# Odd gate and up slabs of the experts: one column group in three one-pass products, six weight slots instead of eight

## The chip, the cores and the metric

The kernel runs on one core of one Trainium2 chip. The metric is the time of one execution on the device in microseconds (us); the median of three executions of the kernel before is 1552.05 us. TensorE (PE) does the matrix products, ScalarE (ACT) and VectorE (DVE) the element-wise work, GpSimd (POOL) some of that and the gathers, and SyncE (SP) issues the weight transfers.

## The reference: what is computed

Two decoder layers over 272 tokens of width 1024. Layer 0 is sliding-window attention and a dense SwiGLU, layer 1 RWKV-7 time mixing and top-2-of-8 SwiGLU experts. The change is in the experts:

```python
def swiglu(t, w_gu, w_down):
    gu = t @ w_gu
    gate, up = jnp.split(gu, 2, axis=-1)
    return (jax.nn.silu(gate) * up) @ w_down

for e in range(N_EXPERTS):                       # 8 experts
    out = out + gates[:, e:e + 1] * swiglu(t, w_gu[e], w_down[e])   # 1024 -> 2 x 3584 -> 1024
```

## The kernel before, in words

The experts run one after the other over at most 96 tokens each, gathered beforehand into `x_all` (the features on the partitions). The 96 tokens are three blocks of 32 (`BLOCKS`). A block's 32 tokens are the stationary operand, so a product fills a strip of 32 columns of TensorE, a **column group** here, and four products that go to the four groups (`quad(j)`, j = 0 to 3) can run beside each other. The weights are the moving operand. All products of the experts are plain float32. In the trace a float32 product shows as two records, each with its own load of the stationary operand; a product of type float32r shows as one.

The weights of one expert come in 24 slabs of 1.8 MB (`BIG`): 16 gate and up slabs (four phases of four slabs: gate and up of the first half of the hidden width, then of the second), and 8 down slabs. A gate or up slab holds two chunks of 128 features (`c`) by four pieces of 448 columns. For each chunk and each block of tokens there are four products, 128x448, one for each column group; I call this a **step**. So a slab has six steps, 24 products and 48 records. Down slabs are multiplied by `hid_T` in products of 256 columns.

The slabs land in `BIG_SLOTS = 8` slots, four in `ring` and four in `arena`. SP issues the load of slab n as soon as slab n - 8 has been multiplied (`big_used`). PE waits for `big_loaded` of the slab's slot. After a gate phase ACT takes the sigmoid (L1687) and DVE multiplies it by the gate (L1773), after the up phase DVE multiplies by up (L1773, `rows_set`) and transposes (L2324, `hidT_set`). In the last expert the 8 down slabs are all resident and are multiplied block by block (`by_block`, L1387), so that the rows of one block are moved out while the next is multiplied; before its end DVE adds the gathered rows of the other experts (`add_rows`, L2278), whose fetches POOL issues (L694), the second one only after `add_rows(0)`.

The engines' queues are in program order, written out by hand; waits stand in the queue where the code has them. L1326 is the helper `pieces` that issues every product of the experts.

Of the kernel before, what the change touches and what calls it, by code (L numbers as in the profile page):

```python
# [20 lines left out]
F32, I32 = mybir.dt.float32, mybir.dt.int32  # L21
# [172 lines left out]
def build(nc, A, OUT):  # L194
    ctx = ExitStack()
    with ctx:
        def sb(name, shape, dtype=F32):
            return ctx.enter_context(nc.sbuf_tensor(name, shape, dtype))
# [136 lines left out]
        otm = [otm, carve(OV + 512 * 23, KC, CH)]  # L335


        x_all = sb("x_all", [P, KC, EXPERTS * CAP])
        hid_T = sb("hid_T", [P, GROUPS, BLOCKS, PIECE])
        hn_hi = sb("hn_hi", [P, TT, D], F32R)  # L340
# [34 lines left out]
        tri = places[:, PASSES * CAP:PASSES * CAP + P]  # L375

        BIG_AT = ARENA - IN_ARENA * BIG
        assert WORK_AT + taken[0] <= BIG_AT and IN_ROWS * BIG <= 2 * TT * D
# [35 lines left out]
        hidT_set = sem("hidden_T_set")  # L414
        big_loaded = [sem(f"expert_slab_loaded{j}") for j in range(BIG_SLOTS)]
        big_used = sem("expert_slab_multiplied")
        hn_ps, hn_hi_set, hn_split = sem("tokens_T_in_psum"), sem("tokens_T_rounded"), sem("tokens_T_split")
        x_ps, x_kept_a, x_kept_v = sem("gathered_in_psum"), sem("gathered_kept_by_scalar"), sem("gathered_kept_by_vector")
        s_early, s_const = sem("vectors_and_eye_loaded"), sem("consts_loaded")
# [280 lines left out]
        def _(pe):  # L700
# [618 lines left out]
            def expert(o, q, e, stored=False):  # L1319
                by_block = e == LAST  # L1320

                def pieces(out, x, w, first, last, blocks=range(BLOCKS)):

                    for b in blocks:
                        for j, piece in w:
                            mm = pe.matmul(out(j, b), x(b), piece, start=first(b), stop=last, skip_group_check=True)  # L1326
                    return mm

                def quad(j):
                    return slice(BLK * j, BLK * (j + 1))  # L1330

                def gate_or_up(i, w):
                    phase, bank = i // PH, 3 * (i // PH % 2)
                    if i == PH:
                        if not e:
                            pe.wait_ge(put_kept, 2 * o + 2)
                        elif not stored:
                            pe.wait_ge(zsum[3], 4 * q - (2 + 4 * LAST))
                    if i % PH == 0 and phase == 2:
                        pe.wait_ge(gate_used, GROUPS * q + 1)  # L1340
                    if i % PH == 0 and phase == 3:
                        pe.wait_ge(rows_set, GROUPS * q + 1)
# [6 lines left out]
                    return mm  # L1349

                def down(i, w, blocks=range(BLOCKS)):
                    if i == 0 and e and 0 in blocks:
                        if stored:
                            pe.wait_ge(y_moved_a, 2 * q)
                            pe.wait_ge(y_moved_v, 2 * q)
                        else:
                            pe.wait_ge(zsum[3], 4 * q - 4 * LAST)
                    first, tiles = BIG // OUT_PIECE * i, {}
                    for x in range(BIG // OUT_PIECE):
                        t, j = divmod(first + x, QUADS)  # L1360
                        tiles.setdefault(t, []).append((j, w[:, OUT_PIECE * x:OUT_PIECE * (x + 1)]))
                    for t, parts in tiles.items():
                        g, c = divmod(t, KT)
                        if c == 0 and parts[0][0] == 0:
                            pe.wait_ge(hidT_set, GROUPS * q + (g + 1))
                        mm = pieces(lambda j, b: PS[quad(j), out_at(b, by_block)[0],
                                                    out_at(b, by_block)[1]:out_at(b, by_block)[1] + OUT_PIECE],
                                    lambda b: hid_T[:, g, b, BLK * c:BLK * (c + 1)], parts,
                                    lambda b: t == 0 and out_at(b, by_block)[1] == 0, t == GROUPS * KT - 1, blocks)
                    return mm  # L1370

                if e == 0:
                    pe.wait_ge(x_kept_a, KC * o + KC)
                    pe.wait_ge(x_kept_v, KC * o + KC)
                for i in range(BIG_GU if by_block else BIG_EXPERT):
                    pe.wait_ge(big_loaded[i % BIG_SLOTS], 16 * BIG_EXPERT // BIG_SLOTS * q + 16 * (i // BIG_SLOTS + 1))
                    w = big[i % BIG_SLOTS]
                    (gate_or_up(i, w) if i < BIG_GU else down(i - BIG_GU, w)).then_inc(big_used, 1)
                    if e == 0:
                        if i == BIG_SLOTS_AT:  # L1380
                            gates_of_slots(o, LAST if stored else 0)
                        if i == BIG_PUT:
                            slots_to_tokens(o, LAST if stored else 0)
                    elif i == BIG_SCATTER and not stored:
                        scatter(q - 1, e - 1, 0)
                        scatter(q - 1, e - 1, 1)
                if by_block:  # L1387
                    for b in range(BLOCKS):
                        for i in range(BIG_GU, BIG_EXPERT):
# [28 lines left out]
        def _(act):  # L1418
# [243 lines left out]
            def keep_gathered(o):  # L1662
                for j in range(0, JOBS, 2):
# [2 lines left out]
                    act.activation(x_all[:, k, HALF * half:HALF * (half + 1)], PS[:, X_BANK[j % 8], 0:HALF],  # L1666
                                   ACT.Copy).then_inc(x_kept_a, 1)

            def expert(o, q, e, stored=False):
                if e and stored:  # L1670
                    move_out(q - 1, e)
                elif e:
# [5 lines left out]
                else:  # L1678
                    act.wait_ge(put_ps, o + 1)
                    for c in range(2):  # L1680
                        act.activation(put[0:CAP, 4 * c:4 * c + 4, :].rearrange("p (b e) t -> p b (e t)", b=2),
                                       PS[0:CAP, 4 + 2 * c:6 + 2 * c, :], ACT.Copy).then_inc(put_kept, 1)
                for g in range(GROUPS):
                    act.wait_ge(big_used, BIG_EXPERT * q + 2 * PH * g + PH)
                    if e or g:
                        act.wait_ge(hidT_set, GROUPS * q + g)
                    act.activation(hid, PS[:, 0:BLOCKS, 0:PIECE], ACT.Sigmoid).then_inc(gated, 1)  # L1687

            def move_out(q, stored=0):
                act.wait_ge(big_used, BIG_EXPERT * q + BIG_EXPERT)  # L1690
# [67 lines left out]
        def _(dve):  # L1758
# [542 lines left out]
            def add_out(q, part):  # L2301
                dve.wait_ge(scattered, 2 * q + (part + 1 - 2 * LAST))
                for t in range(TT):
                    at = z_rows[:, t, GROUP * part:GROUP * (part + 1)]
                    tt(at, at, PS[:, 4 + 2 * part + t, :], ALU.add).then_inc(zsum[3], 1)

            def expert(o, q, e, stored=False):
                if e and stored:
# [8 lines left out]
                for g in range(GROUPS):  # L2317
                    dve.wait_ge(gated, GROUPS * q + (g + 1))
                    tt(hid, hid, PS[:, 0:BLOCKS, 0:PIECE]).then_inc(gate_used, 1)
                    dve.wait_ge(gate_used, GROUPS * q + (g + 1))  # L2320
# [5 lines left out]
                    if e == 0 and g == 0 and stored:  # L2326
                        find_rows(s)
                        assert s.n == RT_ROWS
# [181 lines left out]
```

## Time and profile before

| | |
|---|---|
| median of 3 executions | 1552.05 us (1550.06 to 1552.21) |
| profiled execution, its own time | 1550.99 us |
| its span in the trace | 1549.1 us |
| PE busy | 1501.5 us, 97% of the span |
| experts' products on PE | from 655.3 to 1529.4 us |
| weights of the experts | 192 transfers of 1792 KB |

The span is what the trace shows; 1.9 us lie around it. Matmuls are pipelined, so that a busy PE is not yet PE at its peak. What counts is how fast a slab is multiplied, and what PE waits for between slabs.

### The profile page before, as it was taken

To read this page: it belongs to the slowest core of one execution; us is meant where nothing else is said; L and a number is where in the kernel's file an instruction comes from. 1 tells how busy PE (TensorE), PEld (TensorE's weight loads), DVE (VectorE), ACT (ScalarE), POOL (GpSimd) and SP (SyncE) were. 2 spreads that over 40 slices of the span, in tenths; PEclk is the share of its full clock that TensorE was granted. 3 is DMA by queue.
4 is the path that set the end of the run, shared out by engine and by line. 5 is a ranking of instruction groups with operands and counts; after the bars stand their busy time and mean duration, and the time that the engine had idled before them with its cause. 6 is when DMAs were issued, how large, how long until landed. Compare 5 with 4: busy or idle time off the path is not lost.

```text
span 1549.1 us, 42772 instructions
## 1 busy us (share of the span) xinstructions
PE 1501.5 (97%) x19668; PEld 1090.1 (70%) x19668; DVE 506.7 (33%) x858; ACT 332.9 (21%) x638; POOL 143.8 (9%) x171
## 2 busy tenths in 40 slices
PE   8999999999989998999999999999999999999996
PEld 6778999977989998834656656656557556566553
DVE  4766555476955447511011011110111110110113
ACT  4665444345802223400000000000000000000001
POOL 3330000310014332100000000000000000000000
PEclk9999999999989999999999999999999999999998
DMA  9634555622410003599999999999999999999970
GB/s 264 240 110 136 176 177 167 257 83 82 137 49 4 4 4 110 211 371 410 404 417 407 410 418 404 417 414 405 418 412 403 420 411 406 419 409 409 424 325 30
DMA packets 41378, 432.69 MB, mean 279 GB/s; under 512 B 4919, under 2 KB 5031, under 8 KB 8824
## 3 DMA queue, kind: packets, MB, share of 16 engines
q1 hardware_dynamic: 37672, 417.56, 67.4%
q0 software_dynamic: 3536, 12.51, 2.7%
q8 instruction: 149, 2.44, 0.6%
q14 instruction: 21, 0.17, 0.0%
HBM read 425.95 MB, written 3.87 MB: 277 GB/s over the span
## 4 chain that ended last, share of the span: by engine, by line
PE 71%; DVE 2%; issue 1%; DMA 1%; POOL 1%; ACT 0%; DVEq 0%; SPq 0%
PE PS L1326 55%; PE PS L1095 6%; PE PS L706 6%; PE PS L1114 1%; DMA arena<-in_moe 1%; PE PS L751 1%; PE PS L1266 1%; DVE arena L1773 1%; PE PS L1123 1%; DVE z L1773 0%; PE PS L1212 0%; POOL arena L660 0%; PE PS L1075 0%; PE PS L1239 0%; POOL arena L653 0%
## 5 line engine op out<-in xcount | busy, mean ns | idle before, releaser
L1326 PE MATMUL PS<-ring,x_all 128*32 128x448 f32 x3072 | 298.4, 539 | 0.7 <-issue 0.7
L1326 PE MATMUL PS<-arena,x_all 128*32 128x448 f32 x3072 | 298.0, 539 | 0.0
L1326 PEld LDWEIGHTS PS<-arena,x_all 128*32 128x32 f32 x3072 | 154.2, 110 | 134.8 <-issue 134.8
L1326 PEld LDWEIGHTS PS<-ring,x_all 128*32 128x32 f32 x3072 | 154.3, 110 | 132.4 <-issue 129.8
L1773 DVE TENSOR_TENSOR experts<-experts,PS 128x1344 f32<-128x1344 f32 (+1 forms) x33 | 49.9, 1512 | 499.4 <-ACT experts L1687 255.3
L1326 PE MATMUL PS<-arena,hid_T 128*32 128x256 f32 x2688 | 153.1, 382 | 3.5 <-DMA arena<-in_moe 3.5
L1773 DVE TENSOR_TENSOR w_lo<-ring,w_hi 128x2048 fp32r<-128x2048 f32 x54 | 124.6, 2308 | 86.2 <-PE PS L706 55.6
L1326 PE MATMUL PS<-ring,hid_T 128*32 128x256 f32 x2688 | 151.6, 379 | 0.0
L1326 PEld LDWEIGHTS PS<-arena,hid_T 128*32 128x32 f32 x2688 | 103.2, 111 | 48.7 <-DMA arena<-in_moe 3.9
L1326 PEld LDWEIGHTS PS<-ring,hid_T 128*32 128x32 f32 x2688 | 103.2, 110 | 46.0 <-issue 3.0
L1424 ACT ACTIVATE w_hi<-ring 128x2048 fp32r<-128x2048 f32 x53 | 101.4, 1914 | 137.9 <-issue 82.9
L1095 PE MATMUL PS<-arena 64*64 64x64 f32 (+4 forms) x3296 | 102.9, 216 | 5.4 <-DVE arena L1773 1.5
L1687 ACT ACTIVATE experts<-PS 128x1344 f32<-128x1344 f32 x16 | 20.7, 1292 | 397.1 <-PE PS L1326 397.1
L1095 PEld LDWEIGHTS PS<-arena 64*64 64x64 f32 (+2 forms) x3296 | 96.9, 131 | 10.8 <-issue 4.7
L1695 ACT ACTIVATE experts<-PS 32x256 f32<-32x256 f32 x42 | 15.7, 374 | 372.0 <-PE PS L1326 371.5
L2250 DVE COPY experts<-PS 32x256 f32<-32x256 f32 x42 | 17.7, 422 | 232.2 <-PE PS L1326 231.6
L706 PE MATMUL PS<-h_hi,w_hi 128*128 128x272 f32 x352 | 90.3, 291 | 1.5 <-DVE arena L1773 0.7
L706 PE MATMUL PS<-h_lo,w_hi 128*128 128x272 f32 x352 | 89.3, 288 | 0.0
L686 POOL DMA_DIRECT2D expert_rows<-experts x7 | 3.6, 512 | 785.5 <-DVE experts L2250 785.5
L1773 DVE TENSOR_TENSOR arena<-arena,PS 128x272 f32<-128x272 f32 (+6 forms) x109 | 55.4, 509 | 61.6 <-PE PS L1095 59.8
L706 PEld LDWEIGHTS PS<-h_hi,w_hi 128*128 128x128 f32 x352 | 66.1, 188 | 3.3 <-DVE h_lo L1849 1.6
L706 PEld LDWEIGHTS PS<-h_lo,w_hi 128*128 128x128 f32 x352 | 66.4, 189 | 0.0
(315 smaller groups left out, 1737.7 us busy)
## 6 DMA issues: line engine op xcount, KB each, us to landing
ring<-in_moe SPq DMA_DIRECT2D x96, 1792.0 KB, 9.4
arena<-in_moe SPq DMA_DIRECT2D x96, 1792.0 KB, 9.5
ring<-in_slabs SPq DMA_DIRECT2D x58, 1024.0 KB, 4.9
expert_rows<-experts POOLq DMA_DIRECT2D x7, 384.0 KB, 9.1
arena<-in_lora POOLq DMA_DIRECT2D x1, 1152.0 KB, 5.4
h<-in_h SPq DMA_DIRECT2D x2, 544.0 KB, 5.1
arena<-bias_lines POOLq DMA_DIRECT2D x1, 1056.0 KB, 21.9
arena<-bias_lines POOLq DMA_DIRECT2D x1, 1040.0 KB, 26.7
```

The costliest lines, as they stand in the source:

```text
L706: pe.matmul(out, w, x, start=start, stop=stop)
L751: mm = pe.matmul(PS[:, bank, 0:P], same_head[:, :], ones_d[:, :], start=True, stop=True)
L1095: mm = pe.matmul(PS[64 * p:64 * p + n_out, b + g, at:at + width], lhsT(m, p), rhs(m, p), start=i == 0, stop=i == len(pairs) - 1)
L1114: mm = pe.matmul(out[64 * p:64 * p + CH, :, 0:n], rows_of(x, c)(m, p), r_kk[64 * p:64 * p + 64, :, T * m + START[c]:T * m + START[c] + n], ...
L1123: mm = pe.matmul(PS[64 * p:64 * p + CH, b + g, col + CH * (m % 4):col + CH * (m % 4 + 1)], x(m, p), masks[64 * p:64 * p + 64, MASKS.index( ...
L1266: mm = pe.matmul(PS[:, X_BANK[j % 8], 0:HALF], rows[:, t, P * k:P * k + P], pick[:, t, 4 * half:4 * half + 4, :].rearrange("p e c -> p (e ...
L1326: mm = pe.matmul(out(j, b), x(b), piece, start=first(b), stop=last, skip_group_check=True)
L1424: act.activation(w_hi[:, n % 2, :], ring[:, n % SLOTS, :], ACT.Copy).then_inc(hi_set, 1)
L1687: act.activation(hid, PS[:, 0:BLOCKS, 0:PIECE], ACT.Sigmoid).then_inc(gated, 1)
L1695: a = act.activation(*moved(j, b), ACT.Copy)
L1773: tt = lambda o, a, b, op=ALU.mult: dve.tensor_tensor(out=o, in0=a, in1=b, op=op)
L2250: y = dve.tensor_copy(*moved(j, b))
```

## The change

Of every odd gate and up slab (`SPLIT`: 8 of an expert's 24 slabs, 64 in all) column group 0 no longer multiplies in float32. ACT rounds its two pieces of 448 columns to float32r (`ew_hi`), DVE subtracts to get what the rounding left (`ew_lo`), and the expert's tokens are treated alike once (`xe_hi`, `xe_lo`). Group 0 then sums three products of type float32r: high by high, low by high, high by low. Groups 1 to 3 keep their float32 products. In the code the four groups' products alternate: one of group 0, one float32, and so on.

The new buffers take the place of two slots: six remain, and the load of slab n waits for slab n - 6. In the last expert only the last six down slabs are multiplied block by block, slabs 16 and 17 for all blocks first, and `down` waits there for `rows_set` of the last phase before its first product (a block's output shares a bank with up). `find_rows` and `add_rows` stand after both halves of the hidden width.

```diff
-BIG_SLOTS = 8
+BIG_SLOTS = 6
-IN_ARENA, IN_ROWS = 3, 1
+IN_ARENA, IN_ROWS = 2, 0
+SPLIT = list(range(1, BIG_GU, 2))
...
+                def split_gate_or_up(i):
+                    bank, n, w = 3 * (i // PH % 2), SPLIT.index(i), big[i % BIG_SLOTS]
...
+                    if n == 0:
+                        pe.wait_ge(xe_hi_set, q + 1)
+                        pe.wait_ge(xe_lo_set, q + 1)
+                    for c in range(2):
...
+                        pe.wait_ge(ew_lo_set, 2 * N_SPLIT * q + (2 * n + c + 1))
+                        for b in range(BLOCKS):
+                            rows, at = slice(BLK * b, BLK * (b + 1)), slice(PIECE * c, PIECE * (c + 1))
+                            for j, (x, y) in enumerate([(xe_hi, ew_hi), (xe_lo, ew_hi), (xe_hi, ew_lo)]):
+                                pe.matmul(PS[quad(0), bank + b, 0:PIECE], x[:, k, rows], y[:, at],
+                                          start=False, stop=k == KC - 1 and j == 2, skip_group_check=True)
+                                mm = pe.matmul(PS[quad(j + 1), bank + b, 0:PIECE],
+                                               x_all[:, k, CAP * e + BLK * b:CAP * e + BLK * (b + 1)],
+                                               w[:, PIECE * (QUADS * c + j + 1):PIECE * (QUADS * c + j + 2)],
+                                               start=False, stop=k == KC - 1, skip_group_check=True)
+                        if c == 0:
+                            mm.then_inc(ew_half_used, 1)
...
                 def down(i, w, blocks=range(BLOCKS)):
+                    if i == 0 and by_block:
+                        pe.wait_ge(rows_set, GROUPS * q + GROUPS)
...
-                for i in range(BIG_GU if by_block else BIG_EXPERT):
+                for i in range(BIG_EXPERT - BIG_SLOTS if by_block else BIG_EXPERT):
+                    if i in SPLIT:
+                        split_gate_or_up(i).then_inc(big_used, 1)
...
+            def round_expert_slab(q, e, n, stored):
...
+                        if c == 0:
+                            act.wait_ge(ew_half_used, N_SPLIT * q + n)
+                        else:
+                            act.wait_ge(big_used, BIG_EXPERT * q + (SPLIT[n - 1] + 1 - (0 if n else BIG_EXPERT)))
+                    act.activation(ew_hi[:, at], w[:, of], ACT.Copy).then_inc(ew_hi_set, 1)
...
                 for g in range(GROUPS):
+                    for n in (range(1, 3) if g == 0 else range(3, N_SPLIT - 1)):
+                        round_expert_slab(q, e, n, stored)
...
+            def split_expert_slab(q, n):
...
+                    tt(ew_lo[:, at], w[:, of], ew_hi[:, at].bitcast(F32), ALU.subtract).then_inc(ew_lo_set, 1)
...
-                    if e == LAST and stored:
-                        add_rows(g)
+                if e == LAST and stored:
+                    add_rows(0)
+                    add_rows(1)
```

PE's queue at the start of the first expert, before: slab 0, the products that fetch the tokens' gates, slab 1, the transposes of the picks, slabs 2 and 3.

```order
L1326 MATMUL PS<-ring,x_all 32x448 x24
L1295 MATMUL PS<-gates_split,sq_rounded 96x16 x2
L1326 MATMUL PS<-ring,x_all 32x448 x24
L1304 MATMUL PS<-eye,sq_rounded 96x128 x2
L1326 MATMUL PS<-ring,x_all 32x448 x48
```

The same place now, slab 0 and the first step of slab 1: `ew_` and `xe_` rows are group 0's, the `ring,x_all` rows between them groups 1, 2 and 3.

```order
L1338 MATMUL PS<-ring,x_all 32x448 x24
L1307 MATMUL PS<-gates_split,sq_rounded 96x16 x2
L1376 MATMUL PS<-ew_hi,xe_hi 32x448
L1378 MATMUL PS<-ring,x_all 32x448
L1376 MATMUL PS<-ew_hi,xe_lo 32x448
L1378 MATMUL PS<-ring,x_all 32x448
L1376 MATMUL PS<-ew_lo,xe_hi 32x448
L1378 MATMUL PS<-ring,x_all 32x448
```

So group 0's one product became three, and the other three stand where they stood, one behind each.

DVE's queue in one of the middle experts, before: the rows of the expert before are moved out, then for each half of the hidden width the two multiplications and the transpose.

```order
L2250 COPY experts<-PS 32x256 x6
L1773 TENSOR_TENSOR experts<-experts,PS 128x1344 x2
L2324 STREAM_TRANSPOSE hid_T<-experts 128x1344
L1773 TENSOR_TENSOR experts<-experts,PS 128x1344 x2
L2324 STREAM_TRANSPOSE hid_T<-experts 128x1344
```

The same place now: the tokens' low part, slab 1's, and then the low parts of slabs 3 to 15 between the multiplications.

```order
L1839 TENSOR_TENSOR xe_lo<-x_all,xe_hi 128x768
L1839 TENSOR_TENSOR ew_lo<-ring,ew_hi 128x448 x2
L2316 COPY experts<-PS 32x256 x6
L1839 TENSOR_TENSOR ew_lo<-ring,ew_hi 128x448 x2
L1839 TENSOR_TENSOR ew_lo<-arena,ew_hi 128x448 x2
L1839 TENSOR_TENSOR experts<-experts,PS 128x1344
L1839 TENSOR_TENSOR ew_lo<-ring,ew_hi 128x448 x4
L1839 TENSOR_TENSOR experts<-experts,PS 128x1344
L2408 STREAM_TRANSPOSE hid_T<-experts 128x1344
L1839 TENSOR_TENSOR ew_lo<-arena,ew_hi 128x448 x2
```

Seventeen instructions were added to DVE's queue for each expert, and the multiplication by up now stands behind the four low parts of slabs 7 and 9.

## Rows read from the trace of the kernel before

**Rows 1.** The page: span, busy time and instructions of PE.
```profile
span 1549.1 us, 42772 instructions
PE 1501.5 (97%) x19668; PEld 1090.1 (70%) x19668; DVE 506.7 (33%) x858; ACT 332.9 (21%) x638; POOL 143.8 (9%) x171
```

**Rows 2.** Chain that ended last, in order of time: start us, us, what.
```profile
665.28 822.70 PE PS L1326 x10728
1488.13 13.59 DMA arena<-in_moe
1501.77 27.64 PE PS L1326 x476
```

**Rows 3.** Stretches of expert 1 (gate and up; down): us, PE busy (records), PEclk, DMA share, GB/s.
```profile
769.24:836.88 67.64, 67.64 (x726) 1.00 1.00 415
841.76:868.95 27.19, 27.19 (x508) 1.00 0.99 402
```

**Rows 4.** Timeline of PE where expert 0 ends (`arena,hid_T`) and expert 1 begins (`ring,x_all`).
```profile
763.77 1.07 PE L1326 MATMUL PS<-arena,hid_T 128*32 128x256 f32 x16
764.63 0.55 PE L1326 MATMUL PS<-ring,x_all 128*32 128x448 f32 x2
764.67 0.60 PE L1326 MATMUL PS<-arena,hid_T 128*32 128x256 f32 x4
765.01 1.01 PE L1326 MATMUL PS<-ring,x_all 128*32 128x448 f32 x8
```

**Rows 5.** Groups by form, PE: records | busy us, mean ns | idle before.
```profile
L1326 PE MATMUL PS<-arena,x_all 128*32 128x448 f32 x3072 | 298.0, 539 | 0.0
L1326 PEld LDWEIGHTS PS<-arena,x_all 128*32 128x32 f32 x3072 | 154.2, 110 | 134.8 <-issue 134.8
```

**Rows 6.** Timeline of PE in layer 1's output projection: L758 is float32, L706 float32r.
```profile
621.40 0.70 PE L758 MATMUL PS<-sq,ones_d 128*128 128x256 f32 x2
621.75 0.47 PE L706 MATMUL PS<-out_hi,w_hi 128*128 128x256 f32 x1
622.05 0.28 PE L706 MATMUL PS<-out_lo,w_hi 128*128 128x256 f32 x1
622.17 0.28 PE L706 MATMUL PS<-out_hi,w_hi 128*128 128x256 f32 x1
```

**Rows 7.** Groups of the dense layers that round (ACT) and subtract (DVE).
```profile
L1424 ACT ACTIVATE w_hi<-ring 128x2048 fp32r<-128x2048 f32 x53 | 101.4, 1914 | 137.9 <-issue 82.9
L1773 DVE TENSOR_TENSOR w_lo<-ring,w_hi 128x2048 fp32r<-128x2048 f32 x54 | 124.6, 2308 | 86.2 <-PE PS L706 55.6
```

**Rows 8.** Timeline of ACT and of DVE in expert 1: sigmoid, multiplication by up.
```profile
783.36 1.29 ACT L1687 ACTIVATE experts<-PS 128x1344 f32<-128x1344 f32 x1 [15.72 <-PE PS L1326]
801.47 1.56 DVE L1773 TENSOR_TENSOR experts<-experts,PS 128x1344 f32<-128x1344 f32 x1 [15.23 <-PE PS L1326]
```

**Rows 9.** Slab loads (L519): issued 700 to 1420, 1420 to 1490; all DMA, 1440 to 1490.
```profile
DMA to landing us min/median/max: 8.4/9.4/11.3
DMA to landing us min/median/max: 10.5/12.4/13.6
DMA packets 1931, 21.25 MB, mean 425 GB/s; under 512 B 218, under 2 KB 218, under 8 KB 542
```

**Rows 10.** Timeline of the last expert's down slabs, PE and DVE.
```profile
1487.53 6.03 PE L1326 MATMUL PS<-ring,hid_T 128*32 128x256 f32 x106
1501.77 3.20 PE L1326 MATMUL PS<-arena,hid_T 128*32 128x256 f32 x26 [3.45 <-DMA arena<-in_moe]
1488.07 1.55 DVE L1773 TENSOR_TENSOR experts<-experts,PS 128x1344 f32<-128x1344 f32 x1 [15.23 <-PE PS L1326]
```

**Rows 11.** Timeline of POOL: the first of the second pair of fetches.
```profile
1457.79 0.94 POOL L694 DMA_INDIRECT sq<-expert_rows,row_index  x1 [26.94 <-DVE z L2278]
```

**Rows 12.** The stretch right after PE's wait: us, PE busy, PEclk, DMA share, GB/s.
```profile
1501.53:1504.94 3.41, 3.17 (x32) 0.50 0.10 43
```

**Rows 13.** Timeline of PE: slab 0 of expert 0.
```profile
655.30 4.72 PE L1326 MATMUL PS<-ring,x_all 128*32 128x448 f32 x48 [0.70 <-issue]
```

More of the change, by code:

```diff
@@ L335, in build @@
         otm = [otm, carve(OV + 512 * 23, KC, CH)]
+        EW_HI_AT = KC * EXPERTS * CAP + GROUPS * BLOCKS * PIECE
+        EW_LO_AT = ARENA - (IN_ARENA + 1) * BIG
+        XE_AT = EW_LO_AT - 2 * KC * CAP
+        ew_hi, ew_lo = rounded("ew_hi", EW_HI_AT, [P, 2 * PIECE]), rounded("ew_lo", EW_LO_AT, [P, 2 * PIECE])
+        xe_hi, xe_lo = rounded("xe_hi", XE_AT, [P, KC, CAP]), rounded("xe_lo", XE_AT + KC * CAP, [P, KC, CAP])
         x_all = sb("x_all", [P, KC, EXPERTS * CAP])
@@ L1374, in expert @@
                     pe.wait_ge(x_kept_v, KC * o + KC)
-                for i in range(BIG_GU if by_block else BIG_EXPERT):
+                for i in range(BIG_EXPERT - BIG_SLOTS if by_block else BIG_EXPERT):
+                    if i in SPLIT:
+                        split_gate_or_up(i).then_inc(big_used, 1)
+                        if e == 0 and i == BIG_PUT:
+                            slots_to_tokens(o, LAST if stored else 0)
+                        elif e and i == BIG_SCATTER and not stored:
+                            scatter(q - 1, e - 1, 0)
+                            scatter(q - 1, e - 1, 1)
+                        continue
                     pe.wait_ge(big_loaded[i % BIG_SLOTS], 16 * BIG_EXPERT // BIG_SLOTS * q + 16 * (i // BIG_SLOTS + 1))
@@ L1381, in expert @@
                             gates_of_slots(o, LAST if stored else 0)
[L1382 to L1386, printed above, removed]
                 if by_block:
                     for b in range(BLOCKS):
-                        for i in range(BIG_GU, BIG_EXPERT):
+                        for i in range(BIG_EXPERT - BIG_SLOTS, BIG_EXPERT):
                             if b == 0:
@@ L1667, in keep_gathered, with round_tokens @@
                                    ACT.Copy).then_inc(x_kept_a, 1)
+            def round_tokens(o, q, e, stored):
+                if e == 0:
+                    act.wait_ge(x_kept_a, KC * o + KC)
+                    act.wait_ge(x_kept_v, KC * o + KC)
+                if not (stored and e == 0):
+                    act.wait_ge(big_used, BIG_EXPERT * q + (SPLIT[-1] + 1 - BIG_EXPERT))
+                act.activation(xe_hi[:, :, :], x_all[:, :, CAP * e:CAP * (e + 1)], ACT.Copy).then_inc(xe_hi_set, 1)
+            def round_expert_slab(q, e, n, stored):
+                i = SPLIT[n]
+                w = big[i % BIG_SLOTS]
+                act.wait_ge(big_loaded[i % BIG_SLOTS], 16 * BIG_EXPERT // BIG_SLOTS * q + 16 * (i // BIG_SLOTS + 1))
+                for c in range(2):
+                    at, of = slice(PIECE * c, PIECE * (c + 1)), slice(QUADS * PIECE * c, QUADS * PIECE * c + PIECE)
+                    if n or not (stored and e == 0):
+                        if c == 0:
[3 more added lines that the diff above has]
+                    act.activation(ew_hi[:, at], w[:, of], ACT.Copy).then_inc(ew_hi_set, 1)
             def expert(o, q, e, stored=False):
+                round_tokens(o, q, e, stored)
+                round_expert_slab(q, e, 0, stored)
                 if e and stored:
@@ L2305, in add_out, with split_tokens @@
                     tt(at, at, PS[:, 4 + 2 * part + t, :], ALU.add).then_inc(zsum[3], 1)
+            def split_tokens(q, e):
+                dve.wait_ge(xe_hi_set, q + 1)
+                tt(xe_lo[:, :, :], x_all[:, :, CAP * e:CAP * (e + 1)], xe_hi[:, :, :].bitcast(F32), ALU.subtract)\
+                    .then_inc(xe_lo_set, 1)
+            def split_expert_slab(q, n):
+                w = big[SPLIT[n] % BIG_SLOTS]
+                for c in range(2):
+                    at, of = slice(PIECE * c, PIECE * (c + 1)), slice(QUADS * PIECE * c, QUADS * PIECE * c + PIECE)
+                    dve.wait_ge(ew_hi_set, 2 * N_SPLIT * q + (2 * n + c + 1))
+                    tt(ew_lo[:, at], w[:, of], ew_hi[:, at].bitcast(F32), ALU.subtract).then_inc(ew_lo_set, 1)
             def expert(o, q, e, stored=False):
+                split_tokens(q, e)
+                split_expert_slab(q, 0)
                 if e and stored:
@@ L2317, in expert @@
                 for g in range(GROUPS):
+                    for n in (range(1, 3) if g == 0 else range(5, N_SPLIT - 1)):
+                        split_expert_slab(q, n)
                     dve.wait_ge(gated, GROUPS * q + (g + 1))
                     tt(hid, hid, PS[:, 0:BLOCKS, 0:PIECE]).then_inc(gate_used, 1)
+                    for n in (range(3, 5) if g == 0 else range(N_SPLIT - 1, N_SPLIT)):
+                        split_expert_slab(q, n)
                     dve.wait_ge(gate_used, GROUPS * q + (g + 1))
```

17 lines of the change are left out of this document (13 added, 4 removed).

## The prediction

> **What bounds the kernel now.** I read the page first: PE is busy 97% of the span [rows 1]. Then the chain in order of time: from 665.28 us it is the experts' products without a break, up to one landing of a slab, and products again to 1529.4 [rows 2]. So the question is what bounds PE there, and the stretches say it: in 67.64 us of gate and up slabs PE issues 726 records, 720 of them in the fifteen slabs' own time, 93.9 ns each, at the full clock [rows 3]. A slab of 48 records is 4.51 us, a step of eight records 752 ns.
>
> Now, what is a record worth? Each lasts 539 ns [rows 5], latency included; but 93.9 ns per record times four column groups is 376 ns, and two passes over 448 columns at 2.4 GHz are 373. So every group streams one record at a time, two passes each, without a gap, and a float32 product (two records) keeps its group for 752 ns. The timeline where expert 0 ends shows that the groups are queues of their own. At 764.63 two records of expert 1 (448 columns) start, at 764.67 and after it four of expert 0 (256 columns), which stand ahead of them in the program [rows 4]. Groups 0 and 1 had done their share and went on; 2 and 3 were behind. **A step so lasts as long as its busiest group**, not as long as the sum of its products divided by four.
>
> The Trainium skill says otherwise ("TensorE: Matmul & The Clock Gate", Part 3, what overlaps and what doesn't): matmuls start and end strictly in the order of the program. The trace disagrees here, with these two records at 764.63. I go by the trace; what that rule would give is the last rival.
>
> The loads are not the bound. DMA moves 415 and 402 GB/s in the two stretches [rows 3] but 425 where it has more to do [rows 9]; a slab of 1.835 MB needs 4.32 us of it, and PE asks for one every 4.51. A load lands 9.4 us after its issue, late in the last expert 12.4 [rows 9].
>
> **The change, part by part.**
>
> *Products.* 64 slabs, six steps each: 384 steps. Group 0 had four passes in a step, now three one-pass products: 3 x 187 = 560 ns. Groups 1, 2 and 3 have what they had, 752 ns. The step lasts 752 ns as before, and group 0 idles for a quarter of it. Loading the stationary operand takes 110 ns [rows 5], less than the 187 ns of a pass, beside which it is done. Sum: **0**. One record more per step (nine for eight) has to be issued; two start within some 10 ns of each other [rows 4], eight within 752, so this is hidden as well.
>
> *Unlike types side by side.* Nothing in this trace has a float32r product in a column group of 32, nor one beside a float32 product in another group. The nearest row is on the full array: the second float32 record starts at 621.72, the float32r one behind it is drawn out to 0.47 us, and the next starts at 622.05 [rows 6]: 330 ns for 213 of float32 and 107 of one pass, so 10 ns for the change of type. On group 0 alone that would lie in its slack. From below it is nothing; from above I can't exclude that unlike types shut each other out; both are rivals. I take nothing, the value nearest to the row.
>
> *Rounding and splitting.* ACT needs 0.93 ns a column and DVE 1.13 [rows 7]: 0.42 and 0.51 us for 448 columns, some 0.5 and 0.55 with what a short one costs. The half of a buffer is free when PE is through with it in the odd slab before; the second half at its end. From there 0.5 + 0.55 us and PE needs it a whole even slab, 4.5 us, later. What stands in front in the queues: ACT rounds slab 5 before it takes the sigmoid at the end of gate (1.29 us [rows 8]), half a us late; DVE's low part of slab 9 waits for the end of slab 7 and puts the multiplication by up (1.56 us [rows 8]) 1.2 us later. PE asks for that bank a phase, 18 us, later. In expert 0 the tokens are rounded (768 columns, 0.75 and 0.9 us) from 655.3 on, then slab 1: ready at about 658.5; PE comes to it after 660.0, behind slab 0 [rows 13] and the gates. Sum: **0**; the cover that stays is 2 us in expert 0, over 3 elsewhere.
>
> *Six slots.* A slab's load now has five slabs, 22.5 us, and its rounding 18, against 9.4 to 13.6 us. Hidden, but for the end.
>
> *The end of the last expert.* Call T the end of its slab 15, some 0.3 us before it releases DVE at 1488.07 [rows 10]: 1487.8. Before, PE waited 3.45 us for the last slab [rows 10], and the clock was at 1.2 GHz for 3.41 us behind that wait [rows 12], which costs 1.7 us. Now:
> - The new wait for `rows_set`: DVE multiplies by up from 1488.07 for 1.55 us, and PE used to go on at once, its first groups at 1487.53 [rows 10]. **+2.1 us**, from there to 1489.62.
> - Slabs 16 and 17 take 4.53 us each, then the last six pass at 1.51 each for the first block. Slab 22's load starts behind slab 16, at T + 6.9, slab 23's behind 17, at T + 11.4. PE wants them at T + 17.2 and T + 18.7. At the usual 9.4 us slab 22 lands at T + 16.3 and slab 23 at T + 20.8, 4.4 us behind it: a wait of 2.1. At 8.4 it is 1.1; at 12.4 it is 5.1. The queue is longer in this expert because of the fetches, whose second pair used to start at 1457.79 [rows 11] and now comes behind `add_rows(0)`, which follows DVE's multiplication and transpose: near T + 7 by my estimate, in the midst of these two loads, 1 MB, so 2.4 us of all DMA spread over some 13. I take **2.8 us** for the wait, 0.7 less than before.
> - The clock: a wait of 3.45 us let it fall. Shorter, it may not; I take half of 1.7 us as saved, **-0.8**, bounds -1.7 and 0.
> - `add_rows(1)` ends near T + 24, when the first block is about done. Its rows move out a little late and nobody waits for them before the third block.
>
> Together: 0 + 0 + 2.1 - 0.7 - 0.8 = +0.6 us; bounds 2.1 - 2.4 - 1.7 = -2.0 and 2.1 + 1.6 = +3.7. I forecast +1, the middle between the sum and these bounds: 1550.99 for the profiled execution becomes 1552. The median was 1.06 us above it: **1553.1**.
>
> A measurement of this kernel can tell about 0.2%, 3.1 us, from no change.
>
> **The rivals.**
> - *Friction between unlike types* (slower). Each of the three float32 products of a step now starts behind a one-pass product. At 10 ns each [rows 6], if it falls on the busy groups, 30 ns a step, 384 steps: +11.5 us, 1565. At a few times that, +40. It decides from 8 ns a step. For it: the type does change six times a step; against: 10 ns is at the edge of what I can read, and the groups are separate queues. 0.13.
> - *They shut each other out* (slower). The three passes of group 0 then stand beside nothing: 3 x 187 = 560 ns more a step, +215 us, 1768; with the float32 products in turn too, 3 x (187 + 752) for 752, +790. For it nothing but that no row shows the mixture. 0.09.
> - *A one-pass product isn't one pass in 32 columns* (slower). At two passes group 0 has 3 x 376 = 1128 ns a step: +144 us, 1697. It decides from 250 ns a product. Full-array rows show one pass (117 ns for 256 columns [rows 6]). 0.06.
> - *The groups share their work* (faster). If a free stream took any record, 15 passes would stand for 16: 47 ns a step, -18 us, 1535; DMA would follow (106.2 us for an expert's 44.0 MB is 415 GB/s, below 425 [rows 9]). Two records at 764.63 speak against it [rows 4]: they started before older ones which then had to wait for their own groups. 0.08.
> - *Strictly in order* (faster). If no record started before the one ahead of it, a product's second record, which has to wait 376 ns for its first, would hold back all behind it: four such waits a step before, three now, a quarter less. Of the 752 ns that the rows have [rows 3] a quarter is 188, 72 us in all, 1481. Against it: four such waits with the streams behind them don't fit into 752 ns, and 764.63 [rows 4]. This is what the Trainium skill's rule above (same page and section) would come to. 0.01.
>
> **How the numbers follow.** My forecast has 0.63; within it the end gives less than 3.1 us either way in four of five cases, else more, mostly slower. Slower: 0.13 + 0.09 + 0.06 + 0.10 = 0.38. Faster: 0.08 + 0.01 + 0.02 = 0.11. Within 0.2%: 0.51. The forecast's own range is 1550 to 1556. To leave out no more than 2 in 10 the range takes in shared work and most of the friction: 1534 to 1585; outside lie exclusion, two passes and strict order (0.16) and the worst friction (0.03).
>
> **What would show it.** An odd slab takes 4.51 us like an even one; group 0's one-pass records come at 187 ns in threes and then pause, the others at 376. If odd slabs are at 4.2, work is shared; at 4.7 or more there is friction; at 6.7 group 0 is the bound. No wait of PE on ACT or DVE in between; one of 2 us on DVE at 1488 and one or two on slabs 22 and 23 of the last expert, with or without a fall of the clock. SP's loads land after 8 to 13 us. I am wrong if PE waits for `ew_lo` or for slabs before the last expert, which would say that a queue's order holds more than I followed.

## The result: 1.70 times the time, and the profile after

The changed kernel takes **2633.02 us** (2630.56 to 2634.17, 3 runs) against 1552.05: ratio 1.697, 95% interval 1.695 to 1.699. I had forecast 1553.1 and a range of 1534 to 1585.

The page of the changed kernel, its span, its engines and the costliest groups (busy us, mean ns of one; L1378 is the float32 product of groups 1 to 3 in a split slab, L1376 the float32r product of group 0, L1338 all other products of the experts):

```profile
span 2632.3 us, 43962 instructions
PE 2581.6 (98%) x20052; PEld 1211.6 (46%) x20052; DVE 593.4 (23%) x994; ACT 411.3 (16%) x774; POOL 143.8 (5%) x171
L1378 PE MATMUL PS<-ring,x_all 128*32 128x448 f32 x1728 | 811.3, 551 | 0.0
L1839 DVE TENSOR_TENSOR ew_lo<-ring,ew_hi 128x448 fp32r<-128x448 f32 x96 | 59.2, 624 | 1108.1 <-ACT ew_hi L1728 1108.1
L1338 PE MATMUL PS<-ring,x_all 128*32 128x448 f32 x2304 | 259.6, 540 | 0.7 <-issue 0.7
L1728 ACT ACTIVATE ew_hi<-ring 128x448 fp32r<-128x448 f32 x96 | 54.3, 575 | 1123.9 <-PE PS L1378 933.1
L1376 PE MATMUL PS<-ew_hi,xe_hi 128*32 128x448 f32 x384 | 149.6, 390 | 0.0
ring<-in_moe SPq DMA_DIRECT2D x128, 1792.0 KB, 8.6
```

PE is "98% busy", 97% before, and the durations of the records have hardly moved: a float32 one lasts 551 ns, 539 before [rows 5]. But the 1728 records of L1378 keep PE busy for 811 us, 470 ns each, while 2304 of L1338 need 260, 113 each. Busy time counts a stretch once however many records lie in it, so this is the number to read: at L1338 the records of four groups run side by side, at L1378 those of one product alone. The rest of the change is in order. DVE waits for ACT and ACT for PE, and a load lands after 8.6 us.

The windows of the same trace, one odd slab, the even one behind it and the next odd one:

```profile
core 0: us, PE busy (x) PEld busy (x) DVE busy (x) ACT busy (x) POOL busy (x), PEclk, DMA share, GB/s
687.52:708.93 21.41, 21.41 (x64) 4.40 (x60) 0.63 (x1) 0.58 (x1) 0.00 (x0) 1.00 0.30 115
708.93:713.44 4.51, 4.51 (x49) 1.52 (x42) 2.18 (x2) 1.76 (x2) 0.00 (x0) 1.00 0.65 210
713.44:734.83 21.39, 21.39 (x58) 4.40 (x60) 0.63 (x1) 0.58 (x1) 0.00 (x0) 1.00 0.34 128
```

An odd slab takes 21.39 us where it took 4.51, at the full clock; an even one takes 4.51 still. 64 times 16.88 is 1080 us, and the medians differ by 1081: **the whole loss lies in the odd slabs**. Its timeline in one of them shows how (start, duration; PEld is the loading of the stationary operand; what ended an idle time stands in brackets):

```profile
704.97 0.94 PE L1378 MATMUL PS<-ring,x_all 128*32 128x448 f32 x2
705.84 0.11 PEld L1376 LDWEIGHTS PS<-ew_hi,xe_hi 128*32 128x32 f32 x1 [0.73 <-issue]
705.84 0.39 PE L1376 MATMUL PS<-ew_hi,xe_hi 128*32 128x448 f32 x1
706.16 0.14 PEld L1378 LDWEIGHTS PS<-ring,x_all 128*32 128x32 f32 x2 [0.21 <-issue]
706.16 0.94 PE L1378 MATMUL PS<-ring,x_all 128*32 128x448 f32 x2
```

From one float32 product (a pair of records) to the next are 1.19 us, with one float32r product between them, and three such units make a step: 3.56 us for 752 ns. No two groups overlap. And the operand of the next product is not loaded ahead: PEld starts in the same hundredth of a microsecond as its product, so its 106 ns, hidden elsewhere, now stand in the way each time. PE goes from one unlike product to the next only when the one ahead is all but over: the records overlap by 0.07 us (704.97 + 0.94 is 705.91, the next starts at 705.84), and their ends are modelled.

### The profile page after: what moved, and what is told of

It is laid out like the page before. It is cut to its first block, busy times and chain, and to the rows that moved or that the text cites. A ratio compares the mean times of both kernels' runs of the same rounds, so it can differ in the third digit from the quotient of the medians.

```text
span 2632.3 us, 43962 instructions
## 1 busy us (share of the span) xinstructions
PE 2581.6 (98%) x20052; PEld 1211.6 (46%) x20052; DVE 593.4 (23%) x994; ACT 411.3 (16%) x774; POOL 143.8 (5%) x171
## 4 chain that ended last, share of the span: by engine, by line
PE 83%; DVE 1%; issue 1%; DMA 0%; ACT 0%; POOL 0%; DVEq 0%; SPq 0%
PE PS L1378 38%; PE PS L1338 22%; PE PS L1376 14%; PE PS L1107 3%; PE PS L718 3%; PE PS L1126 1%; PE PS L763 0%; PE PS L1135 0%; PE PS L1278 0%; DVE arena L1839 0%; DMA arena<-in_moe 0%; DVE z L1839 0%; PE PS L1224 0%; PE PS L1087 0%; PE PS L1251 0%
## 5 line engine op out<-in xcount | busy, mean ns | idle before, releaser
L1378 PE MATMUL PS<-ring,x_all 128*32 128x448 f32 x1728 | 811.3, 551 | 0.0
L1839 DVE TENSOR_TENSOR ew_lo<-ring,ew_hi 128x448 fp32r<-128x448 f32 x96 | 59.2, 624 | 1108.1 <-ACT ew_hi L1728 1108.1
L1378 PE MATMUL PS<-arena,x_all 128*32 128x448 f32 x576 | 270.4, 551 | 0.0
L1338 PE MATMUL PS<-ring,x_all 128*32 128x448 f32 x2304 | 259.6, 540 | 0.7 <-issue 0.7
L1728 ACT ACTIVATE ew_hi<-ring 128x448 fp32r<-128x448 f32 x96 | 54.3, 575 | 1123.9 <-PE PS L1378 933.1
L1378 PEld LDWEIGHTS PS<-ring,x_all 128*32 128x32 f32 x1728 | 118.7, 108 | 184.0 <-issue 184.0
L1376 PEld LDWEIGHTS PS<-ew_hi,xe_lo 128*32 128x32 f32 x384 | 40.8, 106 | 281.0 <-issue 281.0
L1376 PEld LDWEIGHTS PS<-ew_lo,xe_hi 128*32 128x32 f32 x384 | 40.7, 106 | 281.0 <-issue 281.0
L1376 PEld LDWEIGHTS PS<-ew_hi,xe_hi 128*32 128x32 f32 x384 | 40.7, 106 | 280.3 <-issue 280.3
L1338 PE MATMUL PS<-arena,hid_T 128*32 128x256 f32 x2688 | 162.1, 382 | 4.4 <-DMA arena<-in_moe 2.7
L1338 PE MATMUL PS<-ring,hid_T 128*32 128x256 f32 x2688 | 153.5, 379 | 0.0
L1338 PEld LDWEIGHTS PS<-ring,x_all 128*32 128x32 f32 x2304 | 88.1, 110 | 134.3 <-issue 132.3
L1376 PE MATMUL PS<-ew_lo,xe_hi 128*32 128x448 f32 x384 | 149.7, 390 | 0.0
L1376 PE MATMUL PS<-ew_hi,xe_hi 128*32 128x448 f32 x384 | 149.6, 390 | 0.0
L1376 PE MATMUL PS<-ew_hi,xe_lo 128*32 128x448 f32 x384 | 148.9, 388 | 0.0
L1338 PEld LDWEIGHTS PS<-arena,hid_T 128*32 128x32 f32 x2688 | 126.2, 110 | 30.7 <-issue 5.2
L1338 PEld LDWEIGHTS PS<-ring,hid_T 128*32 128x32 f32 x2688 | 127.1, 109 | 21.2 <-issue 0.2
```

The source lines that it names most:

```text
L1376: pe.matmul(PS[quad(0), bank + b, 0:PIECE], x[:, k, rows], y[:, at], start=False, stop=k == KC - 1 and j == 2, skip_group_check=True)
L1378: mm = pe.matmul(PS[quad(j + 1), bank + b, 0:PIECE], x_all[:, k, CAP * e + BLK * b:CAP * e + BLK * (b + 1)], w[:, PIECE * (QUADS * c + j + ...
L1728: act.activation(ew_hi[:, at], w[:, of], ACT.Copy).then_inc(ew_hi_set, 1)
L1839: tt = lambda o, a, b, op=ALU.mult: dve.tensor_tensor(out=o, in0=a, in1=b, op=op)
```

## The experiments

All are edits of the changed kernel; "step" is as in the prediction. The numbers are those of the kernels' names (there is no 4). Before ran beside them at 1550.78 us.

**1. Group 0 back to float32.** In the split slabs' loop:

```
-for j, (x, y) in enumerate([(xe_hi, ew_hi), (xe_lo, ew_hi), (xe_hi, ew_lo)]):
-    pe.matmul(PS[quad(0), ...], x[:, k, rows], y[:, at], ...)
-    mm = pe.matmul(PS[quad(j + 1), ...], x_all[...], w[...], ...)
+for j in range(QUADS):
+    mm = pe.matmul(PS[quad(j), ...], x_all[...], w[...], ...)
```

> Group 0 of the split slabs back to one float32 product on the slab itself, in after's code and order; the rounding, the splitting, their waits, six slots and the new end of the last expert stay. Theory 1 (mixing: the whole loss is what float32r products do to the float32 ones around them): the odd slab is 4.51 us again and the time is that of my forecast for the rest, 1550 to 1556 us, with a wait of some 2 us on DVE at the end of up in the last expert. Theory 2 (part of the loss is in the rest: the work of ACT and DVE on the slab, or two slots fewer): above 1560, with waits of PE on ew_lo or on slabs.

Measured: 1554.64 us (11 runs), ratio 1.0017 (1.0006 to 1.0028). Odd slabs take 4.51 us, and PE waits for `ew_lo` nowhere. So the float32r products alone cost 1078 of the 1081 us, and everything else together 2.6 us (0.9 to 4.3) by the ratio; the two medians lie 3.9 us apart.

**2 and 3. Fewer changes of type.** The float32r products of a step first (2), or of half a slab, nine of them (3), and then the float32 ones:

```
 for b in range(BLOCKS):
     for j, (x, y) in enumerate([(xe_hi, ew_hi), (xe_lo, ew_hi), (xe_hi, ew_lo)]):
         pe.matmul(PS[quad(0), ...], x[:, k, rows], y[:, at], ...)
-        mm = pe.matmul(PS[quad(j + 1), ...], x_all[...], w[...], ...)
+for b in range(BLOCKS):          # only in 3; in 2 the same b goes on
+    for j in range(1, QUADS):
+        mm = pe.matmul(PS[quad(j), ...], x_all[...], w[...], ...)
```

> The same products, but in each step the three float32r ones first and then the three float32 ones: two changes between the types a step in place of six. Theory 1 (at each change nothing may be in flight; inside a run of one type the groups overlap): a step is 3 x 187 + 752 + the two changes, 96 + 130 ns, so 1.54 us, +0.79 in 384 steps: +302, about 1855 us. Theory 1b (a pair of one float32r and one float32 product costs 1.186 us whatever its neighbours): 2630 as before.

> The same products, but in each half of a slab the nine float32r ones first, then the nine float32 ones: two changes for three steps. Theory 1: 9 x 187 + 3 x 752 + 226 ns = 4.17 us for what takes 2.26 in float32 alone, +1.91 in 128 halves: +244, about 1797 us. If it comes out with the other order at 1855 too, the changes cost nothing and only the standing alone of the one-pass products counts.

Measured: 1887.87 and 1820.02 us (one run each), 33 and 23 above what I expected, in that order; the 2630 of theory 1b is out. 3 has 256 pairs of changes fewer than 2 and is 67.9 us faster: **265 ns for a pair of changes**. Against the 1554.64 of experiment 1 the half slab of 3 costs 2.07 us more; less one pair, that is 1.81 us for nine one-pass products, 201 ns each. The timeline of 3 at such a change:

```profile
700.66 0.36 PE L1376 MATMUL PS<-ew_hi,xe_hi 128*32 128x448 f32 x1
700.86 0.37 PE L1376 MATMUL PS<-ew_hi,xe_lo 128*32 128x448 f32 x1
700.87 0.11 PEld L1376 LDWEIGHTS PS<-ew_lo,xe_hi 128*32 128x32 f32 x1
701.07 0.36 PE L1376 MATMUL PS<-ew_lo,xe_hi 128*32 128x448 f32 x1
701.36 0.15 PEld L1380 LDWEIGHTS PS<-ring,x_all 128*32 128x32 f32 x6 [0.39 <-issue]
701.36 0.95 PE L1380 MATMUL PS<-ring,x_all 128*32 128x448 f32 x6
```

Inside a run of one kind an operand loads while the product ahead streams (700.87, for the one at 701.07), products of group 0 follow at 0.20 us, and behind the change three float32 products overlap at once (six records in 0.95 us). Between the kinds are 0.29 us and a load that had to wait. Fewer changes save their own cost and restore the overlap of the float32 ones; the time in which group 0 works alone stays.

**5. bfloat16 in group 0** (the order as in the change, six changes of type a step):

```
-pe.matmul(PS[quad(0), ...], x[:, k, rows], y[:, at], ...)
+pe.matmul(PS[quad(0), ...], x[:, k, rows].bitcast(BF16)[:, 1::2], y[:, at].bitcast(BF16)[:, 1::2], ...)
```

> Group 0's three products of a step read the upper halves of the same rounded and low parts as bfloat16 (so these products have 8 bits of mantissa in place of float32r's: that part of the computation is coarser); the order, six changes of type a step and all waits are as in the change. Theory A (float32r is special: one of its products claims all four column groups): bfloat16 products run beside the float32 ones, the step is 752 ns, the time 1550 to 1556 us. Theory B (any change of type empties the array): the step is three units of about 1.19 us again, the time near 2630 us.

Measured: **1554.60 us** (10 runs), ratio 1.0017 (1.0003 to 1.0031), the same as experiment 1. Theory B is out: it isn't that types differ. The timeline, at the border of an even slab (L1339) and a split one (L1377 group 0, L1380 the others):

```profile
771.81 0.36 PE L1377 MATMUL PS<-ew_hi,xe_lo 128*32 128x448 bf16 x1
771.96 0.54 PE L1380 MATMUL PS<-ring,x_all 128*32 128x448 f32 x1
771.97 0.11 PEld L1380 LDWEIGHTS PS<-ring,x_all 128*32 128x32 f32 x1
772.01 0.37 PE L1377 MATMUL PS<-ew_lo,xe_hi 128*32 128x448 bf16 x1
772.02 0.09 PEld L1377 LDWEIGHTS PS<-ew_hi,xe_hi 128*32 128x32 bf16 x1
772.05 0.55 PE L1339 MATMUL PS<-ring,x_all 128*32 128x448 f32 x2
```

Group 0's bfloat16 products at 771.81 and 772.01 are under way while two other groups only start, at 772.05, the last float32 records of the slab before. This is exactly the picture that I had forecast for float32r.

**7 and 9. Does float32r exclude bfloat16 too, and by the product?** In 7 groups 1 to 3 get one bfloat16 product each; in 9 only `xe_hi` by `ew_hi` is float32r and group 0's other two are bfloat16, beside float32:

```
 # 7
-mm = pe.matmul(PS[quad(j + 1), ...], x_all[...], w[...], ...)
+mm = pe.matmul(PS[quad(j + 1), ...], x[:, k, rows].bitcast(BF16)[:, 1::2], y[:, at].bitcast(BF16)[:, 1::2], ...)
 # 9: a, d are x[:, k, rows], y[:, at], and go to group 0's product
+if j:
+    a, d = a.bitcast(BF16)[:, 1::2], d.bitcast(BF16)[:, 1::2]
```

> Group 0's three float32r products of a step as in the change; groups 1 to 3 get one bfloat16 product each from the rounded operands of group 0 in place of their float32 product (their results are other numbers, a third of a split sum). Float32 and float32r are no longer side by side. If a float32r product excludes whatever lies beside it, a step is 3 x 201 + 3 x 187 + 3 x 265 ns, the last the pair of changes as the two orders of the runs before gave it: 1.96 us, +1.21 in 384 steps: about 2015 us. If only float32 and float32r shut each other out, the step is group 0's 561 ns, below what the loads allow: about 1515 to 1530 us.

> Group 0's high by high product stays float32r, its two others become bfloat16 (coarser, as before): one float32r product a step in place of three. If each float32r product costs by itself what it stands alone for, a step is 752 + 201 + 265 ns = 1.22 us: +0.466 in 384 steps over the 1554.6 of bfloat16 alone: about 1734 us, against 2633 for three, so less than a third of the loss, since the float32 products are side by side again between two of them. If one float32r product in a step already serialises all of it: near 2630 us.

Measured: 1979.52 and 1729.90 us (one run each). In 9 one float32r product a step costs 457 ns (175.3 us in 384 steps), 466 expected. In 7, three cost 1.11 us a step, 1.21 expected. A float32r product excludes bfloat16 as it does float32, and pays by itself.

**10 and 11. Why.** In 10 no float32r is left in the odd slabs, and a product 128 columns wide stands in its place; in 11 float32r stands beside wide products:

```
+wide = x[:, :, :].rearrange("p k c -> p (k c)").bitcast(BF16)
+wide = wide[:, 1::2][:, CAP * (k % 4) + BLK * b:CAP * (k % 4) + BLK * b + P]
 # 10: in place of the float32r product of group 0; 11: in place of the float32 ones
+pe.matmul(PS[:, bank + b, 0:PIECE], wide, y[:, at].bitcast(BF16)[:, 1::2], ...)
```

> In place of group 0's three float32r products of a step stand three bfloat16 products whose stationary operand is 128 columns wide: no float32r is left in the odd slabs (their sums are other numbers in all four groups). It asks why float32r excludes the rest. Theory W: a float32r product is carried out on the full width of the array, whatever its 32 columns, and going from full width to 32-column groups and back empties the array. Then a wide bfloat16 product does the same: units of about 1.19 us, time about 2630 us. Theory T: the type does it, and a wide product only has to wait for the streams in its columns, with its operand loaded beforehand: 187 + 752 = 939 ns a unit, +2.07 us in 384 steps: about 2350 us.

> Group 0's three float32r products as in the change; in place of groups 1 to 3's float32 products one bfloat16 product each, 128 columns wide (other numbers, as before). Against the run with float32r beside 32-column bfloat16 (1980 us) only the width of the bfloat16 product differs. Theory W (float32r runs on the full width, so nothing changes between the two): six products of some 200 ns, none drained: 1.2 us a step, +0.45 in 384 steps: about 1725 us, and each operand load starts during the product before. Theory T (the change of type empties the array whatever the widths): 1980 us again or more, and no operand load before the product ahead has ended.

Measured: 2615.91 and 1763.74 us (one run each). The timeline of 10, then that of 11 (L1381 is the wide product there, L1377 float32r):

```profile
699.95 0.94 PE L1381 MATMUL PS<-ring,x_all 128*32 128x448 f32 x2
700.82 0.10 PEld L1379 LDWEIGHTS PS<-ew_hi,xe_hi 128*128 128x128 bf16 x1 [0.73 <-issue]
700.82 0.37 PE L1379 MATMUL PS<-ew_hi,xe_hi 128*128 128x448 bf16 x1
701.12 0.14 PEld L1381 LDWEIGHTS PS<-ring,x_all 128*32 128x32 f32 x2 [0.21 <-issue]
701.12 0.94 PE L1381 MATMUL PS<-ring,x_all 128*32 128x448 f32 x2
```

```profile
700.52 0.10 PEld L1381 LDWEIGHTS PS<-ew_hi,xe_lo 128*128 128x128 bf16 x1 [0.29 <-issue]
700.53 0.37 PE L1381 MATMUL PS<-ew_hi,xe_lo 128*128 128x448 bf16 x1
700.53 0.12 PEld L1377 LDWEIGHTS PS<-ew_lo,xe_hi 128*32 128x32 f32 x1
700.57 0.53 PE L1377 MATMUL PS<-ew_lo,xe_hi 128*32 128x448 f32 x1
700.94 0.10 PEld L1381 LDWEIGHTS PS<-ew_lo,xe_hi 128*128 128x128 bf16 x1 [0.28 <-issue]
700.94 0.37 PE L1381 MATMUL PS<-ew_lo,xe_hi 128*128 128x448 bf16 x1
```

10 repeats the changed kernel's timeline: the same 0.73 and 0.21 us of PEld waiting, 1.17 us a unit, though only bfloat16 and float32 are there. In 11 the operand of the float32r product is loaded as the wide one begins (700.53), so at this change the array isn't emptied ("drained" below), where in 7 it was at every one. A pair takes 0.42 us in the mean; in 7, with a product of 32 columns in the wide one's place, 0.62. The other way, from float32r to the wide product, the operand still comes late in 11. Of the 39 us above what I expected about 20 are this (0.42 for 0.40 us a pair, 18 pairs a slab, 64 slabs), most of the rest lies at the borders to the float32 slabs, where the width does change. Theory W holds against T in both, and the row of before does not speak for T either: there float32 to float32r, both on the full array, cost 10 ns [rows 6]. So **a float32r product behaves as one on the full width of the array, and a change between full width and 32-column groups empties it.**

The Trainium skill has the second half of this ("TensorEngine Tiling (Array Packing)", Tiling Modes, key properties): "Changing tiling mode (not just tile) drains the TensorE". Experiment 10 agrees, with 1.17 us a unit; that a float32r product of 32 columns is such a change rests on experiments 7, 9 and 11 alone.

**6 and 8. What does run side by side.** In 6 all groups take three bfloat16 products from group 0's operands; in 8 every group has its own:

```
-EW_LO_AT = ARENA - (IN_ARENA + 1) * BIG
+EW_LO_AT = EW_HI_AT + BIG // 2
+ew_hi, ew_lo = rounded("ew_hi", EW_HI_AT, [P, BIG], BF16), rounded("ew_lo", EW_LO_AT, [P, BIG], BF16)
-at, of = slice(PIECE * c, PIECE * (c + 1)), slice(QUADS * PIECE * c, QUADS * PIECE * c + PIECE)
+at = of = slice(QUADS * PIECE * c, QUADS * PIECE * (c + 1))
 for m, (x, y) in enumerate([(xe_hi, ew_hi), (xe_lo, ew_hi), (xe_hi, ew_lo)]):
+    for j in range(QUADS):
+        mm = pe.matmul(PS[quad(j), ...], x[:, k, rows], y[:, PIECE * (QUADS * c + j):PIECE * (QUADS * c + j + 1)], ...)
```

> All four groups of the split slabs in three bfloat16 products, all from the rounded operands of group 0 (groups 1 to 3 so get other numbers than theirs). If a bfloat16 product is one pass in every group and the groups overlap, a step is 561 ns and a split slab 3.37 us; the mean of an odd and an even slab, 3.94, is below the 4.32 us that a slab's load needs at 425 GB/s, so the loads bind: an expert takes 103.7 us in place of 108.4, 8 of them save 38 us: about 1516 us. If issuing twelve products and their operand loads within 561 ns is too much (47 ns each), the step is longer; it decides nothing until 700 ns, where PE is the bound again: 1530 to 1555 us.

> The same with every group's own operands: ACT rounds the whole odd slab to bfloat16, DVE writes the rest as bfloat16, each in halves of 1792 columns; both fit where one slab's slot was. Per split slab ACT 3.3 us and DVE 4.0 us in each 8.6 us, so neither is the bound. If they keep ahead of PE: as the run before, about 1516 to 1520 us, the best so far. If the chain landing, rounding, splitting (1.7 + 2.0 us for the first half) makes PE wait without the loads being kept busy: 1525 to 1550 us, with waits of PE on ew_lo and a DMA rate below 420 GB/s.

Measured: 1536.50 us (4 runs; ratio 0.990, 0.989 to 0.992) and **1536.10 us** (4 runs; ratio 0.9906, 0.9890 to 0.9923). Experiment 8 computes the odd slabs from a bfloat16 and its bfloat16 remainder, coarser than float32r's parts, and is faster than both kernels. Its windows, a split slab, a float32 one, and the whole of expert 1; and lines of its groups:

```profile
762.84:766.44 3.60, 3.60 (x80) 3.43 (x76) 0.12 (x1) 1.26 (x1) 0.55 (x1) 1.00 1.01 423
766.44:770.76 4.32, 4.32 (x54) 2.50 (x49) 3.85 (x2) 2.08 (x2) 0.00 (x0) 1.00 1.00 422
762.84:864.89 102.05, 100.95 (x1639) 64.41 (x1634) 40.46 (x24) 30.71 (x22) 0.55 (x1) 1.00 1.01 425
```

```profile
L1839 DVE TENSOR_TENSOR ew_lo<-ring,ew_hi 128x1792 bf16<-128x1792 f32 x96 | 190.1, 2022 | 379.8 <-ACT ew_hi L1728 379.8
L1728 ACT ACTIVATE ew_hi<-ring 128x1792 bf16<-128x1792 f32 x96 | 157.9, 1689 | 421.5 <-DMA ring<-in_moe 401.6 <-PE PS L1379 19.9
L1340 PE MATMUL PS<-ring,hid_T 128*32 128x256 f32 x2688 | 153.8, 382 | 5.1 <-DMA ring<-in_moe 5.1
L1379 PE MATMUL PS<-ew_hi,xe_hi 128*32 128x448 bf16 x1536 | 152.3, 356 | 26.9 <-DVE ew_lo L1839 26.6
```

A split slab now takes 3.60 us, 18 products one after the other in each group at 200 ns, four groups abreast. The loads run at 421 to 425 GB/s without a gap and bind; PE waits 26.6 us for `ew_lo`, which comes late because its slab does (of ACT's 421.5 us idle before rounding 401.6 ended with a load), and 8.5 us for slabs. I had expected 1516 to 1520. Expert 1 takes 102.05 us in place of 108.4, but it lives on slabs that landed ahead. From expert 2 on one takes 106.1 to 106.5. The window of expert 4, and what DMA moves in it:

```profile
1077.86:1183.98 106.12, 102.31 (x1638) 55.07 (x1634) 44.00 (x30) 31.47 (x26) 0.51 (x1) 1.00 1.00 421
DMA packets 3582, 44.64 MB, mean 421 GB/s; under 512 B 401, under 2 KB 401, under 8 KB 497
```

My 103.7 us had the 44.0 MB of the slabs alone at 425 GB/s; 0.6 MB go beside them, and the rate is 421. So an expert gains 2.2 us where I had 4.7. In the last one the chain of waits has

```profile
1408.45 22.34 DMA ring<-in_moe
1440.17 16.55 DMA ring<-in_moe
1476.08 18.67 DMA arena<-in_moe
```

The last slab that PE waits for lands at 1494.8, against 1501.8 before [rows 2], and behind it PE needs 20.05 us where it needed 27.64: 7.0 and 7.6 us, the whole gain.

## Why the prediction was wrong, point by point

- **The step that failed is "Unlike types side by side", with its "I take nothing, the value nearest to the row".** The row was on the full array [rows 6], where both products have the same width, so it couldn't show the cost: a float32r product behaves as a change of the width at which PE works, and on the full array that width doesn't change. The row spoke of another case, not of a near one. 10 ns there is some 250 ns for a pair here, and besides three groups stand still meanwhile.
- **The rival "They shut each other out" came true**, at its worse end, and was undersized. It had 3 x (187 + 752) ns a step; measured are 3 x 1186. The 247 ns between are the changes themselves: in the timeline above the float32r product starts 0.87 us after the float32 one, 0.12 more than its two records need (2 x 373 ns), and the next float32 one 0.32 us later, 0.13 more than one pass. So +790 became +1081. I gave it 0.09, and wrote that nothing spoke for it. True of the trace; but the term carried 384 steps times the whole overlap of four groups, with no row of its own.
- *Products*: right that the operand load and the ninth record of a step are hidden, as far as nothing drains: with bfloat16 in group 0 the step is 752 ns (experiment 5). A one-pass product takes 200 ns in a group, not 187, still far inside. Right, too, against the rival "a one-pass product isn't one pass". "The groups share their work" is refuted by the same run: its 15 passes in place of 16 won nothing. "Strictly in order" too: that would have been faster than before, and products of group 0 start ahead of older ones at 771.81.
- *Rounding and splitting, six slots*: right. ACT 575 ns and DVE 624 (I had 0.5 and 0.55 us), and no wait of PE for them in experiment 1; loads land after 8.6 us in the changed kernel.
- *The end of the last expert*: near. The chain of waits of the changed kernel and the clock around its last wait:

```profile
2570.71 9.75 PE PS L1338 x172
2580.64 10.27 DMA arena<-in_moe
2590.95 21.56 PE PS L1338 x364
```

```profile
2588.00:2590.95 2.95, 0.28 (x4) 0.00 (x0) 2.19 (x2) 0.00 (x0) 0.00 (x0) 0.95 0.98 416
2590.95:2595.00 4.05, 4.05 (x48) 2.04 (x52) 0.48 (x2) 0.47 (x2) 0.00 (x0) 0.62 0.14 59
```

  In experiment 1 the loads that slabs 15 and 16 release, by being multiplied, are issued here:

```profile
1490.16 0.33 SPq L531 DMA_DIRECT2D ring<-in_moe  x1
1497.32 0.33 SPq L531 DMA_DIRECT2D arena<-in_moe  x1
```

  They lie 7.16 us apart, in expert 1 the same two 4.73 (839.64 and 844.37): +2.4 for the wait on `rows_set`, 2.1 forecast. The wait for slabs is 2.7 us, 2.8 forecast; it was 4.3 in experiment 1 and 3.1 in 5, so it varies more than the term does. What I had wrong is the clock: I took half of its cost as saved, and behind the shorter wait it fell all the same (0.62 in the mean of 4.05 us, which costs about 1.5 us).
- The whole rest of the change: +1 forecast, +2.6 (0.9 to 4.3) measured, so "same" would have been right but for the one step. In the one profile of each, the experts start 1.5 us later than before in the changed kernel, 2.0 and 2.8 in experiments 1 and 5, but 0.7 and 1.1 us earlier in 3 and 7, which have the same new buffers. So what lies ahead of the experts scatters by more than the terms at the end are worth, and how the 2.6 us divide isn't settled.
- Of the signs that I had named, the length of an odd slab told it at once, 21.39 us where I had listed 4.2, 4.7 and 6.7. The waits of PE that were to prove me wrong, for `ew_lo` or for slabs before the last expert, never showed: from 687 to 2545 us the trace of the changed kernel has no wait of PE at all. They watched the queues, and the loss came inside PE.

## What to carry to other kernels

When a change puts a kind of product where none stood, ask of each row that is to price it whether it has the same tile width and the same neighbours; if not, its number bounds nothing, and a small experiment or an honest chance has to stand in its place. A PE that is "98% busy" can be four groups or one: divide busy time by records, and look whether an operand is loaded before or with its product. For one-pass products beside 32-column float32 ones take bfloat16 parts, where their accuracy is enough, and keep float32r for full-width stages; before making PE faster, look at how far the loads are behind it, with all that they carry (here 106.1 us an expert, 4.42 a slab, for 4.51).

## What the runs showed of the hardware that I had not expected

- A float32r product in a 32-column group of its own excludes float32 and bfloat16 products in the other groups: 1.19 us for it and one float32 product; bfloat16 in its place costs nothing, and bfloat16 and float32 mix freely in groups. Whether it really streams through the full width, or only sets PE to that mode, no run tells; float32r in groups 1 to 3 wasn't tried.
- A full-width bfloat16 product between 32-column ones drains PE both ways: 1.17 us a unit.
- A change and the change back cost some 220 ns (experiments 7 and 10) to 265 ns (2 and 3), if a one-pass product is taken as 200 ns. The load of the next operand is part of it: it starts with its product (PEld idle for 0.73 and 0.21 us ahead of it), not during the one before.
- From float32r to a full-width bfloat16 product the operand came late as well (0.28 us of PEld idle), though from bfloat16 to float32r it did not. It costs little, 0.42 us for a pair of two 0.20 us products; why the two ways differ is open.
